# Moving the last gelus and their product across a stage boundary, and loading the band mask into the rotation tables' place

## What is computed

```python
for l in range(DEPTH_2):                      # 2 layers, the second is "last"
    hx = x * (1 + sc1) + sh1                  # and hc, the same of the context
    qx, kx, vx, cbx, ccx, cvx, gux, gvx = jnp.split(hx @ w_in[l], SPLIT_POINTS, axis=-1)
    qx = axial_rope(qx...); kx = axial_rope(kx...)
    att_x = window_attention(qx, kx, vx, kc, vc, attn_sink[l])
    o_x = jnp.concatenate([att_x, local_mixers(cbx, ccx, cvx, gux, gvx, ...)], axis=-1) @ w_out[l]
    ...                                       # layer norm, router, experts, layer norm

def local_mixers(cb, cc, cx, gu, gv, conv_w, gm_ws, gm_bs):
    y_conv = cb * short_conv(cc * cx, conv_w)
    u = jax.nn.gelu(gu)
    v = layer_norm(jax.nn.gelu(gv))...
    s = jnp.einsum('gpq,bnqgc->bnpgc', gm_ws, v) + gm_bs...
    y_gm = u * s                              # the product that the change moves
    return jnp.concatenate([y_conv, y_gm], axis=-1)

def window_attention(q, k, v, k_ctx, v_ctx, sink):
    # blocks of 128 queries see 3 x 128 keys under a band mask, and the 256 context keys;
    # the softmax has one more column, the head's sink
```

## Time and profile before

| | us |
|---|---|
| median of 3 runs (lowest to highest) | 2913.95 (2912.28 to 2915.87) |
| the profiled execution | 2918.62 |
| its span, first to last instruction | 2916.8 |
| span in `mixer_inputs`, layers 0 and 1 | from 1157.1 to 1320.9, from 2136.7 to 2257.1 |
| span in `window_attention`, layers 0 and 1 | from 1321.2 to 1413.4, from 2257.4 to 2330.6 |

### The profile page before, as it was taken

How to read it: one execution, slowest core, us unless ns; L and a number is a source line. 1 busy time by engine, 2 the same in 40 slices (tenths; PEclk the granted TensorE clock), 3 DMA queues, 4 the chain that set the end, 5 groups by cost and what they waited for, 6 DMA issues and landing times. The chain is left out here.

```text
span 2916.8 us, 45610 instructions
## 1 busy us (share of the span) xinstructions
PE 2578.5 (88%) x17041; PEld 1732.0 (59%) x17042; DVE 1353.2 (46%) x2641; ACT 616.5 (21%) x1331; POOL 587.7 (20%) x596
## 2 busy tenths in 40 slices
PE   7999999999999999998988989889689885898764
PEld 6877856578886475556655545444357663454332
DVE  6752357427998961346543222222334743232223
ACT  3540158321000012006342000000030722000001
POOL 3432112004442001220203300000113022222101
PEclk9999999999999999998988999999889997899887
DMA  4232320118544743003028889999740326899996
GB/s 146 94 106 87 142 73 30 62 58 239 200 172 177 294 179 127 0 0 152 1 87 326 357 345 421 404 410 397 291 163 9 144 74 282 337 369 389 397 418 239
DMA packets 141485, 597.89 MB, mean 205 GB/s; under 512 B 22705, under 2 KB 43470, under 8 KB 94770
## 3 DMA queue, kind: packets, MB, share of 16 engines
q1 hardware_dynamic: 90144, 361.40, 32.6%
q10 hardware_dynamic: 42530, 213.87, 18.4%
q0 software_dynamic: 8688, 21.00, 2.0%
HBM read 577.26 MB, written 33.75 MB: 209 GB/s over the span
## 5 line engine op out<-in xcount | busy, mean ns | idle before, releaser
L1440 DVE SCALAR_TENSOR_TENSOR psum<-weight_ring,condition_rows 128x1024 f32<-128x1024 f32 x192 | 268.1, 1396 | 16.0 <-issue 0.9
L268 PE MATMUL psum<-weight_ring 128*128 128x256 f32 (+1 forms) x896 | 221.9, 398 | 3.3 <-POOL weight_ring L253 3.3
L3017 PE MATMUL psum<-weight_ring,residual 128*32 128x256 f32 x2176 | 144.4, 411 | 76.4 <-DMA weight_ring<-in_w_dram 47.0
L3006 PE MATMUL psum<-weight_ring,residual 128*64 128x256 f32 x1792 | 205.8, 383 | 0.5 <-issue 0.5
L268 PEld LDWEIGHTS psum<-weight_ring 128*128 128x128 f32 x896 | 170.6, 191 | 43.4 <-issue 4.6
L3006 PEld LDWEIGHTS psum<-weight_ring,residual 128*64 128x64 f32 x1792 | 127.5, 138 | 76.5 <-issue 17.0
L174 PE MATMUL psum<-ffn_hidden,weight_ring 128*128 128x512 f32 (+1 forms) x440 | 154.3, 513 | 4.1 <-DVE ffn_hidden L1485 4.1
L2950 POOL DMA_INDIRECT residual<-token_rows,gather_index x87 | 96.7, 1111 | 295.4 <-issue 277.9
L3017 PEld LDWEIGHTS psum<-weight_ring,residual 128*32 128x32 f32 x2176 | 72.9, 117 | 131.9 <-issue 97.3
L3006 PE MATMUL psum<-third_stream_weights,residual 128*64 128x256 f32 x896 | 116.3, 418 | 38.5 <-DMA third_stream_weights<-in_w_dram 38.5
L174 PEld LDWEIGHTS psum<-ffn_hidden,weight_ring 128*128 128x128 f32 x440 | 84.5, 192 | 73.8 <-issue 69.3
(11 more groups left out here) (538 smaller groups left out, 4677.6 us busy)
## 6 DMA issues: line engine op xcount, KB each, us to landing
third_stream_weights<-in_w_dram ACTq DMA_DIRECT2D x93, 2048.0 KB, 15.3
weight_ring<-in_w_dram SPq DMA_DIRECT2D x84, 2048.0 KB, 18.7
weight_ring<-in_w_ada_dram SPq DMA_DIRECT2D x24, 2048.0 KB, 8.8
weight_ring<-in_w_ffn_dram SPq DMA_DIRECT2D x11, 2048.0 KB, 12.4
weight_ring<-in_w_rnn_dram SPq DMA_DIRECT2D x8, 1536.0 KB, 6.6
weight_ring<-in_w_att_dram SPq DMA_DIRECT2D x6, 2048.0 KB, 8.0
weight_ring<-in_w_in_dram SPq DMA_DIRECT2D x6, 2048.0 KB, 8.8
weight_ring<-in_w_down_dram SPq DMA_DIRECT2D x8, 1408.0 KB, 6.1
```

The lines of the kernel that those rows point to most:

```text
L268: last = c.nc.tensor.matmul(to, weights[:, k * P:(k + 1) * P], rhs[:, k], start=(starts and k == 0), stop=(stops and k == KH - 1), skip_gr ...
L1440: last = v.scalar_tensor_tensor(out=product, in0=w[:, t], scalar=1.0, in1=CR[:, n, :], op0=ALU.mult, op1=ALU.mult, accum_out=c.mod[:, i // ...
L3006: last = nc.tensor.matmul(ps[units.rows(o), 2 + b, 256 * m:256 * (m + 1)], XT[:, b, k % tiles, units.rows(k // tiles)], w[:, k, 256 * o:25 ...
L3017: last = nc.tensor.matmul(ps[units.rows(2 * m + o), 2 + b, 0:256], XT[:, b, k % tiles, units.rows(k // tiles)], w[:, k, 256 * o:256 * (o + ...
```

## The change

- `conv_cx`, a new tensor `sinks` and a new tensor `rope_or_mask` of `[128, 1024]` are allocated by `second_block` ahead of `HX` and kept over both stages. `COS` and `SIN` are the two halves of `rope_or_mask`.
- SyncE loads the sinks with the constants of `mixer_inputs`, which now count seven.
- In `mixer_inputs`, ahead of its first read of pair 4, ScalarE waits until VectorE has made its last rotation and issues the load of the mask into `rope_or_mask`, on its own queue.
- The two gelus and `times(6)` leave `mixer_inputs`. In `window_attention` ScalarE begins with the gelus, and VectorE, after the negated sinks, waits for them, multiplies, waits for the mask (long issued) and goes into the pipeline. ScalarE and GpSimd no longer wait for constants. SyncE begins with the weight ring's loads.
- In `embedding_and_modulate` the two tensors `PT_` and `WR` are placed in free parts of `MIX`.

```diff
@@ embedding_and_modulate
-        PT_ = ctx.enter_context(nc.sbuf_tensor("ple_p", [P, 2, S], F32))
+        PT_ = free[:, KT * S:(KT + 2) * S].rearrange("p (k t) -> p k t", k=2)
+        WR = free[:, (KT + 2) * S:(KT + 2) * S + NL * KT * RW].rearrange("p (l k n) -> p l k n", l=NL, k=KT)
-        WR = ctx.enter_context(nc.sbuf_tensor("router_weights", [P, NL, KT, RW], F32))
@@ mixer_inputs
-        UP, CX = sb("conv_in", [P, 2, UW]), sb("conv_cx", [P, 2, T])
-        COS, SIN, ROT = sb("rope_cos", [P, S]), sb("rope_sin", [P, S]), sb("rope_rot", [P, P])
+        UP, ROT = sb("conv_in", [P, 2, UW]), sb("rope_rot", [P, P])
+        COS, SIN = ROPE[:, 0:S], ROPE[:, S:2 * S]
...
                 sp.dma_start(CW[:, :, :], c.ios["conv2"][l]).then_inc(consts.sem, 16)
+                sp.dma_start(SINK[:, :], c.ios["sink"][l]).then_inc(consts.sem, 16)
...
                 for p, tile in enumerate(PAIRS):
+                    if p == 4:
+                        rot_read.wait(act, nrot)
+                        act.dma_start(ROPE[:, :], c.ios["win_mask"]).then_inc(c.sig("win_consts_landed").sem, 16)
                     read_first(c, act, p, scale_of(tile))
...
-                f.crossed.wait(act, len(PAIRS))
-                nc.scalar.activation(CX[:, 0, width:2 * width], CX[:, 0, width:2 * width], ACT.Gelu_apprx_tanh)
-                nc.scalar.activation(CX[:, 1, 0:2 * width], CX[:, 1, 0:2 * width], ACT.Gelu_apprx_tanh)\
-                    .then_inc(z_read.sem, 1)
...
-                consts.wait(dve, 16 * 6)
+                consts.wait(dve, 16 * 7)
...
                 inner_of(5)
                 outer_of(5)
-                z_read.wait(dve, len(keys) + 1)
-                times(6)
@@ window_attention
             def _(sp):
-                sp.dma_start(MASK[:, :], c.ios["win_mask"]).then_inc(consts.sem, 16)
-                sp.dma_start(SINK[:, :], c.ios["sink"][l]).then_inc(consts.sem, 16)
                 c.ring.feed(sp, c.ring.uses + Ring.SLOTS)
...
             def _(pool):
-                consts.wait(pool, 32)
...
-                consts.wait(dve, 32)
                 v.tensor_scalar(LEAST[:, :], SINK[:, :], -1.0, None, ALU.mult)
-                dve.drain()
+                gated.wait(dve, 1)
+                dve.drain()
+                multiply_rows(c, 6, MIX, CX, parts)
+                landed.wait(dve, 16)
                 pipelined(step, N, TILES)
...
-                consts.wait(act, 32)
+                half = width // 2
+                nc.scalar.activation(CX[:, 0, half:width], CX[:, 0, half:width], ACT.Gelu_apprx_tanh)
+                nc.scalar.activation(CX[:, 1, 0:width], CX[:, 1, 0:width], ACT.Gelu_apprx_tanh).then_inc(gated.sem, 1)
                 pipelined(step, N, TILES)
```

48 lines of the change are left out of this document (28 added, 20 removed).

## The result

In seven executions each, the kernel before took 2915.87 us (median; 2912.28 to 2926.14) and the changed kernel 2900.07 us (2897.28 to 2903.92): a ratio of 0.9944, 95% interval 0.9932 to 0.9955. The changed kernel's profiled execution took 2897.28 us, with a span of 2894.4. Two later jobs (sets of runs taken together) gave 0.9951 [0.9937, 0.9965] and 0.9948 [0.9934, 0.9961]. Over all later jobs the kernel before has a mean of 2917.2 us (72 executions, standard deviation 3.9) and the changed kernel, with its first seven, 2902.4 us (18 executions, 3.0): **14.8 us less**, give or take 1.7. The prediction said 8.34 us less, and 2905.6 us. The direction was right, the size was not. The forecast time lies 3.2 us above the mean of the changed kernel's 18 executions, closer than the saving does, since it starts from a median that was 3.2 us low.

What follows compares the result with a forecast made beforehand. TensorE's matmuls, busy 88% of the span, were taken to bound the kernel, with idle time at two boundaries to win. Savings of 4.73 and 3.61 us, together 8.34, from 2913.95 gave 2905.6 us; 8-in-10 range 2901.5 to 2911.0.

Steps and rivals of the forecast that it cites:

- The boundary chain: From `crossed` to the first mask instruction: 4.73 us earlier in layer 0, 3.61 in layer 1, together 8.34 us.
- the two branches: Behind each boundary, gelus and products (3.67, 2.67 us) beside TensorE's first call (3.75, 2.90 us); the longer was taken.
- Rival 2: TensorE's first call starts no earlier behind the boundary: gain only 2.75 us, time 2911.2 us; chance 0.08.
- Everything costed at nothing: Seventh constant, mask's issue on ScalarE, GpSimd's sink copies and two tensors in `MIX`: each taken as 0 us.
- The step that failed first: At the attention's start, the exponential's table load and scaling follow as before; no gain counted.
- The step that failed second: At both attentions' starts the half clock is mostly put off; losses of 2.5 and 1.5 us kept.
- At most 4.0 us hang on the clock: In the first four steps of both attentions, the low clock loses 2.5 and 1.5 us, no more.
- The step that failed third: From the attention to the end, the length stays as before; the whole gain is let through.
- Rival 1: The clock stays high through the attention's start: gain 12.3 us, time 2901.6 us; chance 0.12.
- Rival 3: Half clock lasts through the later attention steps, costing 12 us: time 2917.6 us; chance 0.04.

Runs made afterwards that it cites:

- unchanged: The kernel before, only a comment changed, run against itself: 2918.71 us, ratio 0.9999.
- moved_tensors: The kernel before with only the embedding stage's two tensors placed in `MIX`: 2918.81 us, ratio 0.9998.
- mask_only: The kernel before with only the early loads of mask and sinks; gelus and products stay in the projections, ScalarE keeps a mask wait: 2912.82 us, ratio 0.9987.
- layer0_only: All parts of the change in layer 0 alone, layer 1 as in the kernel before: 2907.65 us, ratio 0.9956.
- table_back: The changed kernel with one needless ScalarE wait for the mask, putting the exponential's table load back behind its wait: 2907.45 us, ratio 0.9961.
- table_free: The kernel before without ScalarE's wait for the constants, so the exponential's table load runs early: 2910.65 us, ratio 0.9984.
- warm_in_layer_1: The changed kernel with unread matmuls in TensorE's pauses behind its first two calls of layer 1 alone: 2901.77 us, ratio 0.9934.

## Why the prediction was wrong in size

**The boundary chain: right.** Predicted 4.73 and 3.61 us earlier, measured in the pair of traces 4.85 and 3.90 (8.48 to 3.63, and 6.51 to 2.61 or 2.62 by the rows). Boundary 0.35 us, gelus, products and handovers came as costed. The choice between the two branches was the wrong one: TensorE's first call ran at the high clock in both layers, so the products decide, the case that was put at 0.08 and 0.23 us better. In the second layer the high clock is not the change's doing. The prediction took the 2.47 us of one execution for the call; in `unchanged` the same program does it in 1.31 us, after the same pause, and so do `moved_tensors`, `mask_only` and `layer0_only`:

```profile
2249.13 1.31 PE L2102 MATMUL psum<-keys,mix 64*128 64x384 f32 x8 [3.13 <-PEq L1821]
```

Rival 2, a slow entry of TensorE, is out: its first call starts 0.38 and 0.40 us after `crossed`.

**Everything costed at nothing: right.** The seventh constant, the mask's issue (0.39 us, and 7.25 us of idleness behind it), the sinks' copies on GpSimd (four products take 2.00 us beside them instead of 1.96), the tensors in `MIX`.

**The step that failed first: "And after that come the exponential's table load and the scaling, as before."** The load had been counted (none is added), but not where it stands. Its row in the kernel before, released by `win_negmax`, put it on the path behind the first mask instruction. A wait that was listed as removed for its own sake carried it off: 1.35 us at the first exponential, and of the whole 3.9 us by `table_back` and 4.7 us by `table_free`, each give or take some 3. The sum had no term for it. Both directions of the edit agree in that it counts. Whether more is won than the load's own 1.28 us a layer these intervals don't settle. What changes besides is the clock further on: in `table_free` it falls in the second layer's output projection, some 70 us behind the first mask instruction, where the kernel before has no fall.

**The step that failed second: "So the half clock is mostly put off, not avoided, and I keep the loss as it is."** In layer 1 it was right: of the 1.5 us lost in the first four steps, 17.12 - 4 x 3.89 = 1.6 are still lost. In layer 0 it was wrong: 4 x 4.83 = 19.3 us was the pace without loss, and the changed kernel takes 19.21, 18.97 and 18.88, against 21.88, 20.40 and 20.82 in the kernel before. The pause did follow and the clock did fall, but for 7 us instead of 20, 14 and 17. Most of this goes back to the first failed step: the prediction put all that the first steps had lost on the clock ("At most 4.0 us hang on the clock"), but with the table load put back behind its wait they take 20.40 us again, and with it freed alone 19.41, at a lower level as long as in `unchanged`. Nor was 4.0 us the most: the first four steps of the second layer take 14.71 us at the high clock, 0.9 us less than the 15.6 taken as their pace without loss. With the exponential 1.35 us earlier, the transposes follow the second call without a pause (1320.51 above), where TensorE had waited in the kernel before; its timeline there:

```profile
1328.09 3.35 PE L2102 MATMUL psum<-keys,mix 64*128 64x384 f32 x10 [3.52 <-DVE win_negmax L2149]
...
1332.40 2.58 PE L2125 MATMUL psum<-identity,win_probs 128*128 128x128 f32 x11 [0.96 <-ACT win_probs L2172]
```

That this pause is what kept the clock down longer was not tested alone. `table_back`, which has 10 us at half clock there, lies between.

**The step that failed third: "from the attention to the end the same length as before".** Nothing of the work changed there, yet the output projection gained 1.4 us, and the second layer's router 1.0 us in the means of the table (it is less sure: the kernel before has 56.56 us there in one of its traces, 58.18 in another). The last stage's 2.0 us are within its scatter. The clock was costed only where the edit is.

**The rivals.** Rival 1 had a gain of 12.3 us and 2901.6 us, near the time measured, but by luck: the clock did not stay high through the start, and the table load was in no one's sum. Rival 3, slower by a clock that stays low, did not come. By its sum the forecast kept to one profiled execution and to three runs of the kernel before, whose median, 2913.95, was 3 us below the mean of the later 72.

**What stays open.** Why a pause of 2.86 us drops the clock in some kernels and not in others was not found; only that it goes with what the kernel did earlier. Some 15 of the 28 us less at half clock lie outside the two boundaries and are seen only as means over executions. What the lower clock is worth (6.8 us) rests on a correlation: no edit changed the clock alone and was clear of the scatter.

## To carry to other kernels

List the waits of every instruction that the compiler or the language puts in, table loads above all: an activation with two waits can leave one of them on its table load, and a wait that needs nothing, removed, lets the load run early. Cost a closed gap of TensorE at two places, in its own stage and by the low clock behind it, and give the sum a range on the side of the gain for the stages after it. Where executions of one kernel differ by more than the edit is worth, compare stages between marks, and use the mean clock of all timed executions rather than that of one trace.

## What the runs showed of the hardware that was not expected

- TensorE's first call behind a boundary ran at 2.4 GHz after a pause of 0.86 to 0.98 us in all traces of the change; pauses of 2.51 us (layer 1) and 3.50 us (layer 0) right behind that call were each followed by the fall. The length of the pause alone doesn't decide: after 3.13 us at the second boundary the first call took 1.31 us, at 2.4 GHz, in `unchanged`, `moved_tensors`, `mask_only` and `layer0_only` and 2.47 us, at 1.2 GHz, in the kernel before and `table_free`, and a pause of 2.86 us with eight matmuls behind it brought the fall in some kernels and not in others.
- Matmuls that nobody reads, in TensorE's pauses behind its first two calls, kept the clock high through the start of the second attention (1.00 from 2230 to 2290) and made its first four steps 2.5 us shorter. That the whole gains as much was not shown: 1.5 us by the means of `warm_in_layer_1` and the changed kernel, give or take 2.4. In the first attention the same filling only put the fall off.
- A table load of 1.28 us took effect at once, with the activation 0.01 us behind its end.
- A clock that stays high at one place can fall at a later one: `table_free` won 1.95 us in the second attention's first steps and lost 2.3 us in the output projection behind it, at a granted clock of 0.95 instead of 1.00.
